# Sliding-window attention by pairs of heads, with products alternating between halves of the TensorE array

## The reference

```python
N_HEADS, N_KV_HEADS, HEAD_DIM, WINDOW, BLOCK = 16, 4, 64, 128, 128

def sliding_window_attention(q, k, v, sinks):
    ...
    kb, vb = band(k), band(v)            # each block of 128 queries sees its own and the previous 128 keys
    scores = jnp.einsum('bnqhgd,bnkhd->bnhgqk', qb, kb) * (HEAD_DIM ** -0.5)
    ...
    scores = jnp.where(valid[None, :, None, None], scores, NEG_INF_2)
    m = jnp.maximum(jnp.max(scores, axis=-1, keepdims=True), sink)
    p = jnp.exp(scores - m)
    denom = jnp.sum(p, axis=-1, keepdims=True) + jnp.exp(sink - m)
    out = jnp.einsum('bnhgqk,bnkhd->bnqhgd', (p / denom).astype(v.dtype), vb)
```

## Time and profile before

| What | Value |
|---|---|
| Median of three runs | 2287.98 us |
| Profiled execution: span | 2287.2 us |
| TensorE busy | 2208.4 us, 97% |
| VectorE, ScalarE, GpSimdE busy | 880.1, 705.2, 835.9 us |
| Chain that ended last | TensorE 60%, issue 29%, GpSimdE 9% |
| This stage, first scores to the next layer's resumption | 1583.75 to 1771.84 us |

### The profile page before, as it was taken

How to read it: one execution, slowest core, us unless ns; L and a number is a source line. 1 busy time by engine, 2 the same in 40 slices (tenths; PEclk the granted TensorE clock), 3 DMA queues, 4 the chain that set the end, 5 groups by cost and what they waited for, 6 DMA issues and landing times.

```text
span 2287.2 us, 27161 instructions
## 1 busy us (share of the span) xinstructions
PE 2208.4 (97%) x9848; PEld 1751.8 (77%) x9848; DVE 880.1 (38%) x1142; ACT 705.2 (31%) x1063; POOL 835.9 (37%) x347
## 2 busy tenths in 40 slices
PE   8999999999899999999999999999999999999998
PEld 6776666876778787878888878887777887888886
DVE  3654653433567774142221112453333223222111
ACT  4232333333322222233232223223544323322221
POOL 3342211422334444434444433433222443444442
PEclk9999989999999999999999999999999998999999
DMA  5222211211466664223232322322111222332231
GB/s 185 83 92 80 68 37 37 93 46 50 148 210 208 220 219 167 92 74 101 92 101 92 93 91 74 111 92 83 47 47 46 92 93 78 96 94 98 94 99 64
DMA packets 68853, 228.05 MB, mean 100 GB/s; under 512 B 7600, under 2 KB 8880, under 8 KB 68784
## 3 DMA queue, kind: packets, MB, share of 16 engines
q1 hardware_dynamic: 66848, 223.83, 30.2%
q10 hardware_dynamic: 1936, 3.25, 0.5%
HBM read 223.91 MB, written 2.10 MB: 99 GB/s over the span
## 4 chain that ended last, share of the span: by engine, by line
PE 60%; issue 29%; POOL 9%; DVE 1%; ACT 0%; POOLq 0%; DVEq 0%; ACTq 0%
PE bank L1285 12%; PE bank L1286 12%; PE bank L1291 12%; POOL wlo L361 9%; PE bank L1385 5%; PE bank L1387 5%; PE bank L1386 5%; PE bank L1802 2%; PE bank L1815 1%; PE bank L1262 1%; PE bank L1263 1%; PE bank L1264 1%; PE bank L1803 1%; PE bank L1808 1%; PE bank L1423 0%
## 5 line engine op out<-in xcount | busy, mean ns | idle before, releaser
L361 POOL TENSOR_TENSOR wlo<-raw,whi 128x1024 fp32r<-128x1024 f32 x343 | 835.7, 2437 | 1430.0 <-ACT whi L387 1429.8
L1285 PE MATMUL bank<-xh,whi 128*128 128x512 f32 x1664 | 657.2, 395 | 5.2 <-ACT whi L387 5.2
L1286 PE MATMUL bank<-xl,whi 128*128 128x512 f32 x1664 | 651.5, 392 | 0.0
L387 ACT ACTIVATE whi<-raw 128x1024 fp32r<-128x1024 f32 x343 | 362.2, 1056 | 737.6 <-PE bank L1291 419.6
L1291 PE MATMUL bank<-xh,wlo 128*128 128x512 f32 x1664 | 411.3, 390 | 0.0
L1285 PEld LDWEIGHTS bank<-xh,whi 128*128 128x128 f32 x1664 | 314.4, 189 | 73.3 <-issue 5.6
L1286 PEld LDWEIGHTS bank<-xl,whi 128*128 128x128 f32 x1664 | 314.6, 189 | 65.6 <-issue 1.4
L1291 PEld LDWEIGHTS bank<-xh,wlo 128*128 128x128 f32 x1664 | 312.5, 188 | 65.1
L1385 PE MATMUL bank<-hh,whi 128*128 (+1 forms) x528 | 209.1, 396 | 1.3 <-POOL wlo L361 1.3
L1387 PE MATMUL bank<-hh,wlo 128*128 (+1 forms) x528 | 208.6, 395 | 0.0
L1386 PE MATMUL bank<-hl,whi 128*128 (+1 forms) x528 | 208.6, 395 | 0.0
(11 more groups left out here) (251 smaller groups left out, 2277.0 us busy)
## 6 DMA issues: line engine op xcount, KB each, us to landing
raw<-units SPq DMA_DIRECT2D x343, 512.0 KB, 3.5
ada_w<-w_ada SPq DMA_DIRECT2D x96, 384.0 KB, 4.0
h<-x_t SPq DMA_DIRECT2D x8, 256.0 KB, 6.5
dec<-decays ACTq DMA_DIRECT2D x8, 256.0 KB, 2.6
out_t<-h SPq DMA_DIRECT2D x8, 256.0 KB, 2.1
mem_in<-mem_t SPq DMA_DIRECT2D x1, 1024.0 KB, 11.8
kdup<-qkv ACTq DMA_DIRECT2D x8, 128.0 KB, 2.7
tab<-tables SPq DMA_DIRECT2D x1, 832.0 KB, 8.2
```

Source lines behind the costliest of these rows:

```text
L361: pool.tensor_tensor(wlo[:, j % 2 * UNIT:(j % 2 + 1) * UNIT], raw[:, j * UNIT:(j + 1) * UNIT], whi[:, j % 2 * UNIT:(j % 2 + 1) * UNIT].bit ...
L387: act.activation(whi[:, v % 2 * UNIT:(v % 2 + 1) * UNIT], raw[:, slot * UNIT:(slot + 1) * UNIT], ACT.Copy).then_inc(hi_ready, 1)
L1285: mm(bank[:, 0:n], wh, chunk(rhs[0], t, n), start=t == 0, stop=False)
L1286: mm(bank[:, 0:n], wh, chunk(rhs[1], t, n), start=False, stop=False)
```

## The change

The stage is written out by pairs of heads in place of the general `attention` loop.

- Scores: `window_scores(p)` does the four groups of both heads, alternating between the two heads and so between rows 0 to 63 and 64 to 127 of the array; the even head writes banks 0 and 1, the odd one banks 2 and 3. All eight mask products follow behind.
- Values: `window_values(p)` does four products a head, one for each block of keys (256, 256, 256 and 128 queries), alternating between the heads and so between the two halves of output columns, all into bank 6.
- Transposes use banks 4 and 5; `pt_sw` has two buffers.
- Filler: both units of a `cz` pair use bank 7, the gate unit first. ScalarE does the sigmoid after the first; TensorE waits for it (`acted`) before it starts the second, and for VectorE's product (`prod`) before the next pair's first. The two layers' units are swapped in the loaded order.
- TensorE's order for pair `p`: scores of both heads, unit part 0, transposes of the previous pair's first head, part 1, transposes of its second head, the wait, second unit part 0, values of the previous pair, part 1.

```diff
-        pt_sw = at("pt_sw", 5, 896, base=side_at)
+        pt_sw = (at("pt_sw0", 5, 896, base=side_at), at("pt_sw1", 8.5, 896, base=side_at))
...
-        swa = Kind("swa", NSW, SWA_GROUPS, p_sw, pt_sw, HD ** -0.5, [(3, 512, 0), (4, 384, 512)], (6, 7), oh, ol, 0)
+        swa = Kind("swa", NSW, SWA_GROUPS, p_sw, pt_sw, HD ** -0.5, [(4, 512, 0), (5, 384, 512)], (6,), oh, ol, 0)
...
-            attention(swa, pair_evac(swa), conv_filler)
+            def window_exps(hd):
+                act.wait_ge(swa.s_negmax, hd + 1)
+                if hd >= 2:
+                    act.wait_ge(swa.s_tr, hd - 1)
+                p, b0 = swa.p[hd % 2], hd % 2 * 2
+                for q, b, o, w, po in SWA_GROUPS:
+                    act.activation(p[:, po:po + w], banks[b0 + b][:, o:o + w], ACT.Exp,
+                                   bias=nm[:, 4 * hd + q:4 * hd + q + 1], scale=swa.scale,
+                                   accum_out=sm[:, 4 * hd + q:4 * hd + q + 1]).then_inc(swa.s_exp, 1)
+                act.activation(es[:, 4 * hd:4 * hd + 4], nm[:, 4 * hd:4 * hd + 4], ACT.Exp,
+                               bias=col("sinks", hd)).then_inc(swa.s_sink, 1)
+            def window_probabilities_copy(hd):
+                act.wait_ge(swa.s_tr, hd + 1)
+                if hd >= 2:
+                    act.wait_ge(swa.s_pv, hd // 2)
+                act.activation(swa.pt[hd % 2][:, 0:512], banks[4][:, :], ACT.Copy).then_inc(swa.s_pt_act, 1)
+            pairs_n = NSW // 2
+            for p in range(pairs_n + 1):
+                split_ahead(L["cz"].u0 + 2 * p)
+                if p >= 1:
+                    window_probabilities_copy(2 * p - 2)
+                if p < pairs_n:
+                    window_exps(2 * p)
+                    act.wait_ge(unit_used, L["cz"].u0 + 2 * p + 1)
+                    if p >= 2:
+                        act.wait_ge(prod, PROD["cz"] + p - 1)
+                    act.activation(chunk(tmp, p % 2), banks[7][:, :], ACT.Sigmoid).then_inc(acted, 1)
+                if p >= 1:
+                    window_probabilities_copy(2 * p - 1)
+                if p < pairs_n:
+                    split_ahead(L["cz"].u0 + 2 * p + 1)
+                    window_exps(2 * p + 1)
+                if p >= 1:
+                    act.wait_ge(swa.s_pv, p)
+                    act.activation(chunk(oh, p - 1), banks[6][:, :], ACT.Copy).then_inc(swa.s_hi, 1)
...
-            attention(swa, None, pair_evac(swa), conv_filler)
...
+            pairs_n = NSW // 2
+            for p in range(pairs_n + 1):
+                if p >= 1:
+                    dve.wait_ge(acted, ACTED["cz"] + p)
+                    dve.wait_ge(unit_used, L["cz"].u0 + 2 * p)
+                    tt(chunk(m1, p - 1), chunk(tmp, (p - 1) % 2), banks[7][:, :], ALU.mult).then_inc(prod, 1)
+                if p < pairs_n:
+                    window_maxima(2 * p)
+                    window_maxima(2 * p + 1)
+                if p >= 1:
+                    window_probabilities_copy(2 * p - 2)
+                if p < pairs_n:
+                    window_normalise(2 * p)
+                if p >= 1:
+                    window_probabilities_copy(2 * p - 1)
+                if p < pairs_n:
+                    window_normalise(2 * p + 1)
+                if p >= 1:
+                    dve.wait_ge(swa.s_hi, p)
+                    tt(chunk(ol, p - 1), banks[6][:, :], chunk(oh, p - 1).bitcast(f32), ALU.subtract).then_inc(swa.s_lo, 1)
...
+            def window_scores(p):
+                g = 2 * p // (NSW // NKV)
+                for n, (q, b, o, w, _) in enumerate(SWA_GROUPS):
+                    qq, k0 = (4 + p) * T + q * P, g * T + (q + 1) * P - w
+                    for r in range(2):
+                        r0 = r * HD
+                        mm(banks[2 * r + b][:, o:o + w], qkv[r0:r0 + HD, qq:qq + P], kdup[r0:r0 + HD, k0:k0 + w],
+                           start=o == 0, stop=False, skip_group_check=True)
+                for r in range(2):
+                    for q, b, o, w, _ in SWA_GROUPS:
+                        last = mm(banks[2 * r + b][:, o:o + w], mask16[:, 0:P], mask16[:, 3 * P - w:3 * P],
+                                  start=False, stop=True, skip_group_check=True)
                 return last
-            def swa_transposes(hd):
-                for n, (q, kb) in enumerate(SWA_PAIRS):
-                    last = nc.tensor.transpose(banks[3 + n // 4][:, n % 4 * P:(n % 4 + 1) * P], swa.p[hd % 2][:, n * P:(n + 1) * P], ident)
-                return last
-
-            def swa_values(hd):
-                r0, g = hd % 2 * HD, hd // (NSW // NKV)
-                bank = banks[6 + hd // 2 % 2]
-                for n, (q, kb) in enumerate(SWA_PAIRS):
-                    last = mm(bank[r0:r0 + HD, q * P:(q + 1) * P], v_sw[:, kb * 256 + g * HD:kb * 256 + (g + 1) * HD],
-                              swa.pt[:, n * P:(n + 1) * P], start=q == 0 or kb < q, stop=kb == q)
-                return last
+            def window_transposes(hd):
+                pe.wait_ge(swa.s_pn, 4 * hd + 4)
+                if hd >= 1:
+                    pe.wait_ge(swa.s_pt_act, hd)
+                    pe.wait_ge(swa.s_pt_dve, hd)
+                for n in range(len(SWA_PAIRS)):
+                    last = nc.tensor.transpose(banks[4 + n // 4][:, n % 4 * P:(n % 4 + 1) * P],
+                                               swa.p[hd % 2][:, n * P:(n + 1) * P], ident)
+                last.then_inc(swa.s_tr, 1)
+            def window_values(p):
+                pe.wait_ge(swa.s_pt_act, 2 * p + 2)
+                pe.wait_ge(swa.s_pt_dve, 2 * p + 2)
+                if p >= 1:
+                    pe.wait_ge(swa.s_lo, p)
+                g = 2 * p // (NSW // NKV)
+                for kb in range(QB):
+                    q1 = min(kb + 2, QB)
+                    for r in range(2):
+                        r0 = r * HD
+                        last = mm(banks[6][r0:r0 + HD, kb * P:q1 * P], v_sw[:, kb * 256 + g * HD:kb * 256 + (g + 1) * HD],
+                                  swa.pt[r][:, 2 * kb * P:(kb + q1) * P], start=kb == 0, stop=kb == QB - 1,
+                                  skip_group_check=True)
+                last.then_inc(swa.s_pv, 1)
+            def unit_part(u, rhs, part):
+                slot = u % 2
+                if part == 0:
+                    pe.wait_ge(hi_ready, u + 1)
+                    high_passes(slot, range(6), banks[7], rhs, T)
+                else:
+                    high_passes(slot, (6, 7), banks[7], rhs, T)
+                    pe.wait_ge(lo_ready, u + 1)
+                    low_pass(slot, banks[7], rhs, T).then_inc(unit_used, 1)
             swa_first = held(7)
-
-            def conv_unit(hd, half):
-
-                if hd == NSW:
-                    if half == 0:
-                        pe.wait_ge(swa.s_exp, 4 * NSW)
-                    two_units(L["az"].u0, [(oh, ol), X], (swa.s_lo, 0), swa_first[half], (0,))
-                if hd < NSW:
-                    if hd == 0 and half == 0:
+            pairs_n = NSW // 2
+            all_banks_taken()
+            for p in range(pairs_n + 1):
+                if p < pairs_n:
+                    if p >= 1:
+                        pe.wait_ge(swa.s_exp, 8 * p)
+                    window_scores(p).then_inc(swa.s_scores, 1)
+                    if p == 0:
                         pe.wait_ge(half_lo, HALVES["b"] + C)
-                    if hd >= 2 and half == 0:
-                        pe.wait_ge(prod, PROD["cz"] + hd // 2)
-                    u = L["cz"].u0 + hd
-                    half_unit(u, u % 2, banks[5 if hd % 2 else 2], X if hd % 2 else Y, T, half)
-            attention(swa, swa_scores, swa_transposes, swa_values, pair_out_free(swa), fill=conv_unit)
-            bank_free[2] = bank_free[5] = [(prod, PROD["cz"] + C)]
-            for b in (0, 1):
+                    else:
+                        pe.wait_ge(prod, PROD["cz"] + p)
+                    unit_part(L["cz"].u0 + 2 * p, X, 0)
+                else:
+                    pe.wait_ge(swa.s_exp, 4 * NSW)
+                    two_units(L["az"].u0, [(oh, ol), X], (swa.s_lo, 0), swa_first[0], (0,))
+                if p >= 1:
+                    window_transposes(2 * p - 2)
+                if p < pairs_n:
+                    unit_part(L["cz"].u0 + 2 * p, X, 1)
+                if p >= 1:
+                    window_transposes(2 * p - 1)
+                if p < pairs_n:
+                    pe.wait_ge(acted, ACTED["cz"] + p + 1)
+                    unit_part(L["cz"].u0 + 2 * p + 1, Y, 0)
+                else:
+                    two_units(L["az"].u0, [(oh, ol), X], (swa.s_lo, 0), swa_first[1], (0,))
+                if p >= 1:
+                    window_values(p - 1)
+                if p < pairs_n:
+                    unit_part(L["cz"].u0 + 2 * p + 1, Y, 1)
+            bank_free[7] = [(prod, PROD["cz"] + C)]
+            bank_free[6] = [(swa.s_lo, 8)]
+            for b in range(4):
```

(41 more changed lines are left out.)

25 lines of the change are left out of this document (2 added, 23 removed).

## The result

The changed kernel takes 2252.01 us (median of 4 runs, 2250.77 to 2255.07) against 2288.18 for the kernel before, a ratio of 0.9848 with the 95% interval 0.9834 to 0.9862. A second set of runs of the same kernel gave 2253.51 us and 0.9855 (0.984 to 0.987). The profiled execution has a span of 2248.9 us, 38.3 less than before.

The account below looks back on a forecast made before the run. TensorE was taken as the bound; first pass 15.6 plus 1.41 of half clock, seven pairs 135.1 and tail 13.6 make 165.7 us against 188.1, saving 22.4: 2265.5 us forecast, range 2253 to 2286.

Parts of the forecast that it names:

- What bounds the kernel: TensorE, busy 97% of the span and 176.00 of 176.00 us in the stretch: only its own time can be won.
- Grouping: Scores and values: fewer shape changes (0.32 us each there and back) and merged products save 1.9 us per pair.
- the scores: Scores of both heads with masks, halves fully overlapped: 3.1 us per pair, against 2 x 2.93 before.
- the values: Values of both heads, column halves fully overlapped: 1.88 us per pair, against 3.34 before.
- The new wait: TensorE waits for ScalarE's sigmoid between the units sharing bank 7: 1.3 us per pair, bounds 0.6 and 2.
- The sum: All block times and waits of the stage: 19.3 us a pair against 22.16, stage 165.7 against 188.1, saving 22.4.
- the first pass of the loop: First pair, without the previous pair's transposes and values: 15.6 us including a 0.8 stall, plus 1.41 of half clock kept.
- the tail: Last transposes and values among the next layer's first tiles: 13.6 us, including a new 0.94 wait for copies.
- A: Scores and values: the halves don't overlap, so only 4.0 us is saved, 2284; chance 0.15.
- Rival C: Scores and values: each of 112 alternations between halves costs 0.20 us, 22 us in all, so slower, 2306; chance 0.13.
- B: Scores and values: overlap in one kind alone, by half, or full with the clock halved at times: 2272 to 2279; chance 0.22.
- D: Less stall (7 x 0.7) and score streams of 1.47 (8 x 0.4), 8 us more saved: 2257; chance 0.08.

Follow-up runs that it names:

- head by head: Changed kernel, with all even-head products before all odd-head products in scores and values: 2266.57 us, ratio 0.9911 to the kernel before.
- alternating by two: Changed kernel, with two products of the even head, then two of the odd, in turn: 2254.19 us, ratio 0.9851 to the kernel before.
- by three: Changed kernel, with three products of the even head, three of the odd, then one each: 2260.11 us, ratio 0.9878 to the kernel before.

## Why the prediction was right, and where it was off

**What bounds the kernel** held: what was taken from TensorE's row came out of the stage: the blocks and the wait add up to 3.90 us per pair, and the period fell by 3.84.

**Grouping** was right in its price. The fixed share of 0.32 us, worked out as a difference of two groups, came back as 0.31 when it was put in again. Eight masks take 0.70 us, which is their stream alone; 0.86 was in the sum (0.70 and eight times 0.02). Behind each other they have no fixed share at all, the lower bound.

The fp32 part of the scores takes 1.72 us for sixteen passes, which is what eight take for one head in the kernel before with its masks grouped (1630.40 to 1632.12). The terms of the sum that were mis-sized are the scores, 2.42 for 3.1 (1.72 to the first mask where 1.9 + 0.32 stood, and 0.70 of masks for 0.86), and the values, 1.67 for 1.88.

**The new wait** was foreseen in its place, cause and size: idle 0.97, and from the transposes' start to the unit's start 1.89 us where 0.68 + 1.3 = 1.98 stood. It was cured as its working says.

**The sum.** A pair is 18.32 us for 19.3: 0.68 from scores, 0.21 from values, 0.09 from the wait. Over seven periods that is 6.9 us; the first pass of the loop took 14.6 for 15.6, the tail 13.2 for 13.6. The 1.4 us of half clock kept in the sum didn't come: both profiles of before have a stretch of 3.4 us at half clock with the first head, and none of the changed or grouped ones has. Whether the shorter first block of 64-row products keeps it away was not tried apart. These terms make 6.9 + 1.0 + 0.4 + 1.4 = 9.7, against the 9.6 us by which the stage's gain was under-forecast (32.0 for 22.4). The time came out at the lower edge of the range because of these, and in the first pair of profiles another 6.3 us outside the stage, which no term stood for, came on top.

**Rivals.** A fell with the paired starts and the run head by head. Rival C fell with them: 112 changes of half cost nothing. B (clock halved each pair) didn't occur: the granted clock is 1.00 through the stage, in spite of 9.6 idle microseconds (0.69 in the first pair, seven times 0.97, 0.74 and 1.42 in the tail). D's time, 2257, was nearer than the forecast's own; its cause for the scores, streams at their full 1.47, was right (half of 2.94), its other cause, a shorter stall, was not. The rule of the Trainium skill that was cited (TensorEngine Tiling (Array Packing), Key Properties: changing the tiling mode drains the array and changing the tile doesn't, tiles load and compute in parallel) agrees with the trace in both halves: 0.31 us for a change of shape, 6 ns between loads and between passes of two halves.

**The range** was cut too tight below: it took the best case of the stall and streams together as 8 us and gave it 0.08, and had no term for the half-clock stretches in the rest of the program, which alone moved the stage's start by 3.5 us between two profiles of one kernel.

## What to carry to other kernels

Two small products that use different row or column halves of the array cost the time of one here if they stand near each other in the order, and it needn't be strict: alternating by two costs 0.10 us more in a block of scores and 0.05 in one of values. Put products of one shape together, for a change of the array's shape cost 0.31 us here, there and back, and ask what the shortened stretch was covering: here one chain (sigmoid behind a table load) and one product became late, and moving a block of transposes by six passes gave back another 7.5 us of the stage. When one engine is full, its block sums from start to start predicted within 0.1 us per block what was not new to the trace.

## What the runs showed of the hardware that was not expected

TensorE started fp32 passes of the other half out of the program's order, past up to three waiting passes; with four or more waiting, it didn't (head by head, by three). Where both halves have a pass and its weights ready, the starts lie 5 to 14 ns apart (5 to 7 alternating, 12 to 14 by two). This holds for row halves (scores) and for column halves of one PSUM bank (values). Sixteen passes alternating take 1.72 us, by two 1.83, by three 2.05, head by head 2.48 to the first mask. Masks in bf16 behind each other take 0.11 us for 256 columns and 0.06 for 128, load of the weights included.
